# Attention in a hybrid encoder: mixing in two passes a key tile, denominators added up on POOL

## What is computed

```python
s = (einsum('bqhd,bkhd->bhqk', qn, k_nope) + einsum('bqhd,bkd->bhqk', qr, k_rope)) * scale
p = softmax(s, axis=-1)                    # 8 heads, 64 + 32 features of q and k
out = einsum('bhqk,bkhd->bqhd', p, v)      # 64 values a head
```

## Time and profile before

| | us |
|---|---|
| median of 3 runs (3899.96 to 3902.69) | 3901.63 |
| the profiled execution | 3902.54 |
| its span in the trace | 3900.7 |
| granted clock over the span, of full speed | 0.957 |
| attention: first unit to last output | 901 to 1866 |

### The profile page before, as it was taken

The page is one execution under the profiler, slowest core; times in us unless marked ns, Lnnn a source line. Parts: engine busy times, 40 slices in busy tenths (PEclk is TensorE's granted clock), DMA queues, the critical chain, the costliest instruction groups (busy, mean ns, idle before and its releaser), DMA issues. The chain is left out here.

```text
span 3900.7 us, 51502 instructions
## 1 busy us (share of the span) xinstructions
PE 3562.4 (91%) x19453; PEld 2993.5 (77%) x19453; DVE 2219.5 (57%) x3813; ACT 1532.4 (39%) x1959; POOL 204.4 (5%) x122
## 2 busy tenths in 40 slices
PE   5999969986999999999599839999999999999991
PEld 4888858874777777777478638999999999999991
DVE  4444457766777777776454454555454555555545
ACT  2111134443666666666322203333333333333335
POOL 0000000000000000000011100110000000000100
PEclk9999989997999999999899859999999999999995
DMA  2112145656112222110333214555555555555546
GB/s 104 59 59 74 53 155 203 216 210 140 36 24 53 53 53 55 34 25 7 135 133 129 92 63 152 170 161 165 171 159 174 156 157 176 159 173 157 160 130 240
DMA packets 314711, 470.46 MB, mean 121 GB/s; under 512 B 79072, under 2 KB 215008, under 8 KB 311904
## 3 DMA queue, kind: packets, MB, share of 16 engines
q1 hardware_dynamic: 302816, 426.94, 34.7%
q0 software_dynamic: 11776, 41.95, 5.0%
HBM read 352.83 MB, written 116.00 MB: 120 GB/s over the span
## 5 line engine op out<-in xcount | busy, mean ns | idle before, releaser
L63 PE MATMUL psum<-xeT_hi,w_hi 128*128 128x320 f32 x2048 | 635.4, 310 | 0.0
L64 PE MATMUL psum<-xeT_lo,w_hi 128*128 128x320 f32 x2048 | 633.6, 309 | 0.0
L65 PE MATMUL psum<-xeT_hi,w_lo 128*128 128x320 f32 x2048 | 633.6, 309 | 0.0
L1892 ACT ACTIVATE w_hi<-w_raw 128x2048 fp32r<-128x2048 f32 x192 | 358.6, 1907 | 295.5 <-PE psum L65 199.5
L1970 DVE TENSOR_TENSOR w_lo<-w_raw,w_hi 128x2048 fp32r<-128x2048 f32 x192 | 432.2, 2285 | 40.2 <-ACT w_hi L1892 40.2
L1210 ACT ACTIVATE p_hi<-psum 128x1024 fp32r<-128x1024 f32 x272 | 279.1, 1026 | 360.5 <-PE psum L65 360.5
L1246 DVE TENSOR_REDUCE mx<-psum 128x1 f32<-128x1024 f32 x256 | 313.5, 1225 | 161.3 <-PE psum L1136 161.3
L63 PEld LDWEIGHTS psum<-xeT_hi,w_hi 128*128 128x128 f32 x2048 | 385.2, 188 | 1.0
L64 PEld LDWEIGHTS psum<-xeT_lo,w_hi 128*128 128x128 f32 x2048 | 385.3, 188 | 0.6
L65 PEld LDWEIGHTS psum<-xeT_hi,w_lo 128*128 128x128 f32 x2048 | 385.2, 188 | 0.0
L1264 DVE TENSOR_TENSOR p_lo<-p_raw,p_hi 128x1024 fp32r<-128x1024 f32 x272 | 333.3, 1225 | 82.8 <-ACT p_raw L1212 79.5
(11 more groups left out here) (323 smaller groups left out, 6840.6 us busy)
## 6 DMA issues: line engine op xcount, KB each, us to landing
w_raw<-in_w_gate SPq DMA_DIRECT2D x64, 1024.0 KB, 6.1
w_raw<-in_w_up SPq DMA_DIRECT2D x64, 1024.0 KB, 7.7
w_raw<-in_w_down SPq DMA_DIRECT2D x64, 1024.0 KB, 5.4
rec<-rec SPq DMA_DIRECT2D x20, 768.0 KB, 3.7
recb<-rec SPq DMA_DIRECT2D x20, 768.0 KB, 5.1
xa<-in_x SPq DMA_DIRECT2D x20, 512.0 KB, 4.4
xb<-in_x SPq DMA_DIRECT2D x20, 512.0 KB, 5.9
xo<-in_x SPq DMA_DIRECT2D x20, 512.0 KB, 3.4
```

Source lines behind the costliest of these rows:

```text
L63: pe.matmul(out, a[0], b[0], start=first, stop=False)
L64: pe.matmul(out, a[0], b[1], start=False, stop=False)
L65: return pe.matmul(out, a[1], b[0], start=False, stop=last)
L1892: a.activation(w_hi[n % 4][:], raw[n % 4][:], ACT.Copy).then_inc(s["hi_made"], 1)
```

## The change

1. **Mixing.** v_lo and v_hi lie side by side in one buffer, with ones behind. A key tile takes two matmuls: [v_lo, v_hi] (128 columns) against p_hi into bank 4, and [v_hi, ones] (65 columns) against p_lo into bank 7.
2. **Denominators.** The sum of p_hi is no longer a column of the matmul. POOL adds up the p_hi of a block's slots (7 additions of 128x1024 in a prompt block, 1 in a sample block) and folds the two key tiles together once a block. ACT's p_hi buffer is free again only when POOL has read it.
3. **p_lo from PSUM.** The second exponential is written over the scores in PSUM, after a wait for the first; DVE subtracts from there. The score banks are free again after DVE's subtraction, not after ACT.
4. **Output.** ACT copies banks 4 and 7 out in slot last+1; in slot last+2 `sum_out` adds the parts with twelve fp32 matmuls (three for each of four groups of 128 queries) into bank 6.
5. **Order and banks.** Row and output now use the units' banks 5 and 6. PE in slot g: score, row, output sum, mix, unit. ACT: copies, row, exponentials. DVE: output, reduce, make_lo. The first eight units use three pairs of banks by turns.
6. **Constants** are written by POOL.
7. **Backward tail.** From step 21 on the pairs go round seven buffers; the four new ones lie where `x_hi` and `x_lo` were.

```diff
+        pair += [t[:, 1, b * D:(b + 1) * D].rearrange("p (a n) -> p a n", a=2) for t in (cq_hi, cq_lo) for b in range(2)]
...
+            late = n - pair_no.get((NT + 1, "V"))
+            home[n] = n % 3 if late < 0 else (late + 3) % 7
+            uses[n] = used[home[n]]
+            used[home[n]] += 1
+
+        def wait_home(eng, n):
+
+            if home[n] > 2:
+                eng.wait_ge(s["lat_projected"], NT)
+            wait_from_one(eng, pair_out[home[n]], 16 * uses[n])
 
         with nc.Block() as block:
...
                     a.wait_ge(s["filled"], n + 1)
-                    if m >= 3:
-                        a.wait_ge(pair_out[m % 3], 16 * (m // 3))
-                    a.activation(pair[m % 3][:, 0, :], ps[:, 6 + n % 2, :], ACT.Copy).then_inc(s["pair_hi_made"], 1)
+                    wait_home(a, m)
+                    a.activation(pair[home[m]][:, 0, :], ps[:, 6 + n % 2, :], ACT.Copy).then_inc(s["pair_hi_made"], 1)
 
...
+    VW = 2 * MV + 2
+    B_O, B_O2, B_ROW, B_OUT = 4, 7, 5, 6
...
-        vals = [(sb(f"v_hi{b}", [P, NT, MV + 1], F32R), sb(f"v_lo{b}", [P, NT, MV + 1], F32R)) for b in range(2)]
-        p_raw = [sb(f"p_raw{b}", [P, 2, 512]) for b in range(2)]
+        vals = [sb(f"v_lo_hi{b}", [P, NT, VW], F32R) for b in range(2)]
...
-        oT = sb("oT", [MV + 1, 512])
+        o_hi, o_lo = sb("o_hi", [2 * MV, 512]), sb("o_lo", [MV + 1, 512])
+        added = [sb(f"added{b}", [P, 2, 512]) for b in range(2)]
+        added_up = [sb(f"added_up{b}", [P, 512]) for b in range(2)]
+        fold, ones = sb("fold", [2 * MV, MV + 1]), sb("ones_col", [P, 1])
...
+        last_of = [g0 + (7 if qb < 4 else 1) for g0, h, qb in starts]
+        out_slot = {g + 2: n for n, g in enumerate(last_of)}
+        adds_before, n_adds = [], 0
+        for g0, h, qb in starts:
+            adds_before.append(n_adds)
+            n_adds += 7 if qb < 4 else 1
+
+        def wait_added(eng, g):
+
+            n = block_no(g)
+            eng.wait_ge(s["p_added"], adds_before[n] + max(g - starts[n][0], 1))
+
+        def unit_bank(n):
+
+            return (5, 0, 2)[n % 3] if n < 8 else 5
...
-                        sp.dma_start(vals[b][w][:, :, 0:MV].bitcast(F32), d["v"][w, :, :, MV * h:MV * (h + 1)].rearrange("t p e -> p t e")
+                        sp.dma_start(vals[b][:, :, (1 - w) * MV:(2 - w) * MV].bitcast(F32),
+                                     d["v"][w, :, :, MV * h:MV * (h + 1)].rearrange("t p e -> p t e")
...
-                    wait_from_one(pe, s["unit_reduced"], n)
+                    wait_from_one(pe, s["unit_reduced"], n if n >= 8 else n - 2)
+                    wait_from_one(pe, s["row_made"], sum(1 for g in row_slot if g <= n - AHEAD))
+                    wait_from_one(pe, s["o_made"], sum(1 for g in out_slot if g <= n - AHEAD))
...
-                            pe.wait_ge(s["constant_rows"], h + 1)
-                    wait_from_one(pe, s["raw_made"], g - 1)
+                            pe.wait_ge(s["constant_rows"], 4 * (h + 1))
+                        if h == 0:
+                            pe.wait_ge(s["unit_reduced"], 8)
+                    wait_from_one(pe, s["lo_made"], g - 1)
...
-                        wait_from_one(pe, s["oT_made"], block_no(g))
+                        wait_from_one(pe, s["o_copied"], block_no(g))
+                    pe.wait_ge(s["hi_made"], g + 1)
+                    for z in range(2):
+                        pe.matmul(ps[:, B_O, :], vals[b][:, key_tile(j) + z, 0:2 * MV], p_hi[g % 4][:, z, :],
+                                  start=first and z == 0, stop=last and z == 1)
                     pe.wait_ge(s["lo_made"], g + 1)
                     for z in range(2):
-                        t = key_tile(j) + z
-                        ins = mm3(pe, ps[0:MV + 1, 4, :], (vals[b][0][:, t, :], vals[b][1][:, t, :]),
-                                  (p_hi[g % 4][:, z, :], p_lo[g % 4][:, z, :]), first and z == 0, last and z == 1)
+                        ins = pe.matmul(ps[0:MV + 1, B_O2, :], vals[b][:, key_tile(j) + z, MV:2 * MV + 1],
+                                        p_lo[g % 4][:, z, :], start=first and z == 0, stop=last and z == 1)
                     ins.then_inc(s["mixed"], 1)
 
-                def turn_row(n):
+                def turn_row(n, units):
                     pe.wait_ge(s["mx4_made"], n + 1)
-                    wait_bank7(pe, "row", n)
+                    pe.wait_ge(s["unit_reduced"], units)
                     for q in range(4):
-                        ins = pe.matmul(ps[0:1, 7, q * P:(q + 1) * P], mx4[n % 2][:, q:q + 1], c.ident,
+                        ins = pe.matmul(ps[0:1, B_ROW, q * P:(q + 1) * P], mx4[n % 2][:, q:q + 1], c.ident,
                                         start=True, stop=True)
                     ins.then_inc(s["row_turned"], 1)
 
-                def turn_out(n):
-                    pe.wait_ge(s["oT_made"], n + 1)
-                    wait_bank7(pe, "out", n)
+                def sum_out(n, units):
+
+                    pe.wait_ge(s["o_copied"], n + 1)
+                    pe.wait_ge(s["p_added_up"], n + 1)
+                    wait_from_one(pe, s["o_made"], n)
+                    pe.wait_ge(s["unit_reduced"], units)
+                    if n == 0:
+                        pe.wait_ge(s["fold_made"], 3)
                     for q in range(4):
-                        ins = pe.transpose(ps[:, 7, q * (MV + 1):(q + 1) * (MV + 1)], oT[:, q * P:(q + 1) * P],
-                                           c.const[0:MV + 1, C_ID:C_ID + MV + 1])
-                    ins.then_inc(s["out_turned"], 1)
-
-                for g in range(-AHEAD, TOTAL + 1):
+                        cols = slice(q * P, (q + 1) * P)
+                        at = q * (MV + 1)
+                        pe.matmul(ps[:, B_OUT, at:at + MV + 1], o_hi[:, cols], fold[:], start=True, stop=False)
+                        pe.matmul(ps[:, B_OUT, at:at + MV + 1], o_lo[:, cols], c.const[0:MV + 1, C_ID:C_ID + MV + 1],
+                                  start=False, stop=False)
+                        ins = pe.matmul(ps[:, B_OUT, at + MV:at + MV + 1], added_up[n % 2][:, cols], ones[:],
+                                        start=False, stop=True)
+                    ins.then_inc(s["out_summed"], 1)
+
+                for g in range(-AHEAD, TOTAL + 2):
                     if 0 <= g + LATE < TOTAL:
                         score(g + LATE)
+                    if g in row_slot:
+                        turn_row(row_slot[g], g + AHEAD)
+                    if g in out_slot:
+                        sum_out(out_slot[g], min(g + AHEAD, TOTAL))
+                    if 0 <= g < TOTAL:
+                        mix(g)
                     if g + AHEAD < TOTAL:
                         unit(g + AHEAD)
-                    if g in row_slot:
-                        turn_row(row_slot[g])
-                    if 0 <= g < TOTAL:
-                        mix(g)
-                    if g in out_slot:
-                        turn_out(out_slot[g])
 
...
-                    wait_from_one(a, s["mixed"], g - 3)
+                    if g >= 4:
+                        a.wait_ge(s["mixed"], g - 3)
+                        wait_added(a, g - 4)
                     a.activation(p_hi[g % 4][:], src, ACT.Exp, scale=MSCALE).then_inc(s["hi_made"], 1)
-                    wait_from_one(a, s["lo_made"], g - 1)
-                    a.activation(p_raw[g % 2][:], src, ACT.Exp, scale=MSCALE).then_inc(s["raw_made"], 1)
+                    a.wait_ge(s["hi_made"], g + 1)
+                    a.activation(src, src, ACT.Exp, scale=MSCALE).then_inc(s["raw_made"], 1)
...
-                def take_out(n):
-                    g0, h, qb = starts[n]
-                    a.wait_ge(s["mixed"], g0 + (8 if qb < 4 else 2))
-                    wait_from_one(a, s["out_turned"], n)
-                    a.activation(oT[:], ps[0:MV + 1, 4, :], ACT.Copy).then_inc(s["oT_made"], 1)
-
-                for g in range(-AHEAD, TOTAL + 1):
-                    if g in out_slot:
-                        take_out(out_slot[g])
+                def copy_out(n):
+                    a.wait_ge(s["mixed"], last_of[n] + 1)
+                    wait_from_one(a, s["out_summed"], n)
+                    a.activation(o_hi[:], ps[:, B_O, :], ACT.Copy)
+                    a.activation(o_lo[:], ps[0:MV + 1, B_O2, :], ACT.Copy).then_inc(s["o_copied"], 1)
+
+                for g in range(-AHEAD, TOTAL + 2):
+                    if g - 1 in last_of:
+                        copy_out(last_of.index(g - 1))
+                    if g in row_slot:
+                        take_row(row_slot[g])
                     if 0 <= g + LATE < TOTAL:
                         exponentials(g + LATE)
-                    if g in row_slot:
-                        take_row(row_slot[g])
+
+            @block.gpsimd
+            def _(g):
+                n = 0
+                for b in range(2):
```

(46 more changed lines are left out.)

46 lines of the change are left out of this document (18 added, 28 removed).

## The result

The changed kernel takes 3951.1 us, median of 4 runs (3946.2 to 3953.5); the kernel before, run beside it, 3900.8. The ratio is 1.0125, 95% interval 1.011 to 1.014: slower by 50 us. The forecast was 3932 with a range of 3880 to 3960. The profiled execution of the changed kernel took 3946.2 us, its span is 3944.4, 43.7 longer than the span before.

A forecast was written before the change was run, and what follows sets the result against it. Attention was taken to be bound by what PE issues. Gains of 136.6 us against losses of 165.7 gave +29 on the profiled execution's 3902.5, forecast 3932 us, range 3880 to 3960.

The forecast's parts named there:

- Mixing: Six mixing matmuls of an attention slot become four: 3.25 to 2.79 us, 120.6 gained, 2.5 more in the last slots.
- DVE's two long operations fit the slot: In a plain slot, maximum and subtraction fit, under 0.1 us spare; the rival that they don't: 3958 us, chance 0.10.
- Output sum: In slot last+2, twelve fp32 matmuls replace four transposes: +2.4 us x 40 blocks, 96 us lost (88 to 104).
- Copies: In slot last+1, ACT's two copies out delay the next block's mixing: 0.72 us x 31, 22 lost (9 to 30).
- the 0.6 to 0.8 that I wanted to see: Sign for the forecast: PE idle 0.6 to 0.8 us after score at each block start, released by ACT's copy.
- Row and mx4: Before each of 39 rows of maxima, PE starts 0.25 us later (10 us); POOL's addition holds mx4 0.9 (35 us).
- The sign that I named: mx4 starting where a POOL addition ends would show the forecast right; mx4 starting inside one would show it wrong.
- Start and backward tail: Attention's first score at about 918.5, gain 10.5 us (6 to 12); seven buffers in backward tail, gain 3 (0 to 7).
- End: At the end, two copies for one and twelve matmuls for four on a bare path: 2.7 us lost.
- mx4 not held: Rival: POOL does not hold mx4 before a row; 35 us less, 3897 us, chance 0.20.
- POOL and the subtraction exclude each other: Rival: in attention they cannot overlap, a slot lasts 3.6 us, 186 us more, 4118 us, chance 0.02.
- The waits at the borders don't arise: Rival at block borders: second exponential under about 0.65 us, copy and row about 10, with mx4 free 3875 us, chance 0.16.

The follow-up runs named there:

- the two runs above: Changed kernel with DVE's two small operations before a row as one-operand reductions: 3924.8 us; changed kernel with POOL adding only each block's first pair: 3929.6 us.
- the run with `p_raw`: Changed kernel with the second exponential written into SBUF and the subtraction for p_lo reading two SBUF operands: 4008.8 us (ratio 1.0288).

## Why the prediction was right, and where it was not

The sign, the range and the mechanism held: PE bound attention, mixing gave what was counted, and the output sum took most of it back. The median came out 19 us above the forecast. Against the profiled execution, for which the sum was made, it is 14.6 of span (43.7 for 29), and the median of the runs lies another 4.9 above that execution, the fastest of the four (its granted clock is 0.954 over the span, that of the others 0.951 or 0.952). The 14.6 are 13.7 of clock, -0.9 in the loop, +2.3 at its end, -1.5 at the start, +1.0 in the rest. That the loop comes within 0.9 is in part luck: the output sum was priced 10 us too low and the row 8 too high. By its steps:

- **Mixing.** Predicted 3.25 to 2.79 a slot; 3.24 to 2.77. The last slots take 2.32 and 2.81 by turns, 2.56 on average, predicted 2.55 (its own terms, 3.6 and 1.39 for two slots, give 2.50). DVE's two long operations fit the slot: no wait for them in plain slots.
- **Output sum.** Predicted 2.4 more a block, measured 2.65. The price of a matmul, taken from the router's rows, was 0.2125 and came out at 0.20 to 0.25; the start was 0.18 behind the score, not 0.1. Over the 38 sums inside the exponentials' span that is 101 us in place of 91. Leaving out four matmuls or doubling all twelve moved the time by about this price, once the clock is set apart.
- **Copies.** Predicted 0.72 in 31 blocks, 22 us; measured 0.65 in 32, 21 us. Only 0.4 of it stands as idle time of PE, not the 0.6 to 0.8 that I wanted to see: by the distances of starts PE is held 0.54 us (0.77 from the last score matmul to mixing, for 0.23), but the last score matmul's own 0.39 covers part of that, and the first pair of mixing matmuls takes 0.10 more than elsewhere. The cause was shown by putting a unit in front.
- **Row and mx4.** Predicted 0.25 + 0.9 = 1.15; measured 0.95, of which the two runs above give 0.7 to the hold and 0.25 to the row's place. 37 us in place of 45; PE stands 0.8 us before a row, 1.0 in the two-slot blocks, not over 1. The lock, which was inferred from a kind of meeting that no row showed, is shown: the form of the operation and POOL's standing still each remove it. The Trainium skill ("SBUF — State Buffer", section "SBUF: two separate sides") calls it an exclusive lock between a GpSimd operation and a DVE operation with two SBUF inputs or in a two-port mode. These runs agree: 0.85 to 0.16 us for the two-operand form, 1.02 to 0.16 for the copy, which had but one operand. The copy would fall under the second half of the rule; no row shows in which mode it ran. The prediction priced mx4 as an operation on two operands throughout, though in the eight two-slot blocks it is this copy. The sign that I named was wrong, though: I wrote that mx4 would start where an addition ends, and that a start inside an addition would refute the step. It starts inside and is stretched.
- **Start and backward tail.** Predicted 10.5 and 3; measured 10.9 and 4.1 by landmarks, 13.4 together in a run of their own. These hold to some 3 us: in the thirteen traces of kernels with this start the first exponential starts anywhere from 914.4 to 920.5.
- **Clock.** This is the step that was missing: the sum priced every edit at the clock of before, 1.00 throughout attention, and had no term for it. 27.3 us at half clock cost up to 13.7 us, nearly the whole miss of the profiled execution. The fall follows the output sum, so it belongs to that edit's price.
- **End.** Predicted 2.7, and two of the 40 output sums (4.8) lie in this stretch too: 7.5; measured 9.8. The last slots of the changed kernel, ACT and PE:

```profile
1894.43 0.59 ACT L1262 ACTIVATE o_lo<-psum 65x512 f32<-65x512 f32 x1
...
1895.08 0.73 PE L1193 MATMUL psum<-p_hi,v_lo_hi 128*128 128x512 f32 x2 [2.21 <-ACT o_lo L1262]
...
1898.80 0.67 PE L1220 MATMUL psum<-fold,o_hi 128*128 128x65 f32 x2
...
1900.08 1.20 PE L1193 MATMUL psum<-p_hi,v_lo_hi 128*128 128x512 f32 x2
```

The copies of one block and the mixing of the next follow each other on a bare path (2.21 us of idle PE), and 1.1 us into the first sum, at 1897.2, the clock falls to half: mixing that showed 0.63 shows 1.20. The last two sums ran at half clock for the most part, where the step counted full. Here the idle time stands ahead of the fall too, so this place doesn't tell which of the two brings it.

Of the rivals, "mx4 not held" and "POOL and the subtraction exclude each other" are both decided: the first is false, the second false with p_lo read from PSUM and true with p_lo read from SBUF. "The waits at the borders don't arise" failed because the second exponential takes 1.01 us, not under 0.65.

## What to carry to other kernels

A saving in the inner loop must be set against what it asks for once per block: here 0.47 us x 8 slots were bought with 2.65 + 0.95 + 0.65 us a block, and the remedy was in the block's border (one bank, one copy, eight matmuls, a unit in front of a wait), not in the loop. When work is moved to POOL, list every DVE operation that touches SBUF alone, tiny ones too, and write each in a form that isn't held; one that is merely moved keeps its cost, since the next thing in DVE's queue inherits it.

## What the hardware showed that I had not expected

- **A held DVE operation has no wait in the trace.** It shows as duration: 850 ns for 4 columns that take 161 otherwise. In reading a profile, the duration of tiny operations is to be compared with that of the same ones where POOL stands still.
- **The clock fell without a long gap of PE.** Inside attention the granted clock fell to half in every profile of a kernel with twelve matmuls in the output sum (4 to 10 stretches), in 38 with twenty-four, and in none with eight, whether PE had gaps of 0.4 to 1.0 us beside them or hardly any. Each of the stretches with twelve began 2.1 to 3.5 us after such a sum, 2.6 to 2.7 us long, had begun, so the sum is what they follow; why only some of the 38 sums are followed by one isn't settled.
- **An exponential of 128x1024 written over its own PSUM input takes 1008 ns.** The same one into SBUF takes 1026 ns in the run with `p_raw`, and 1018 in the kernel before, where it doesn't wait for the first.
